# Computing the modulation vectors of a two-block network with column-grouped matmuls instead of row sums on VectorE

## The reference

```
def modulation(cvec, w, b):
    m = jax.nn.silu(cvec) @ w + b
    return jnp.split(m, 3, axis=-1)

def modulate(n, shift, scale):
    return n * (1.0 + scale) + shift
...
        shift, scale, gate = modulation(c, mod_w[i], mod_b[i])
        h = modulate(rmsnorm(x, norm_g[i]), shift[:, None], scale[:, None])
        ...
            shift_c, scale_c, gate_c = modulation(c_ctx, mod_w[i], mod_b[i])
        ...
        x = x + gate[:, None] * y
```

## Time and profile before

| what | us |
|---|---|
| median of 3 runs | 3019.34 (3016.89 to 3021.15) |
| the profiled execution, its own time | 3007.58 |
| span of the profiled execution | 3005.8 |
| PE busy | 2610.2 (87%) |
| PE weight loads busy | 2028.2 (67%) |
| DVE busy | 1748.8 (58%) |
| ACT busy | 1122.0 (37%) |
| POOL busy | 776.2 (26%) |

### The profile page before, as it was taken

One profiled execution on the slowest core, in us unless ns is written; L12 is line 12 of the kernel. 1 busy time (PEld: TensorE's weight loads), 2 busy tenths in 40 slices (PEclk: granted clock), 3 DMA queues, 4 the chain that ended last, 5 costly groups with the idle time before them and its releaser, 6 DMA issues. The chain is left out here.

```text
span 3005.8 us, 65971 instructions
## 1 busy us (share of the span) xinstructions
PE 2610.2 (87%) x28252; PEld 2028.2 (67%) x28252; DVE 1748.8 (58%) x2951; ACT 1122.0 (37%) x1751; POOL 776.2 (26%) x437
## 2 busy tenths in 40 slices
PE   7896879998599997788888888678999999898987
PEld 5774658776487686677677777567778755476755
DVE  4646978977822675454554554354771066535995
ACT  4531332223333422444444443332442344333323
POOL 2322210001122123644444452122332300032111
PEclk9998989989698898899999999889999999999998
DMA  4214424432234455111111100324332200033431
GB/s 149 77 43 133 161 71 118 111 93 91 97 107 151 157 188 182 40 36 45 51 40 46 51 25 14 122 91 147 133 126 64 84 1 1 1 119 92 136 94 56
DMA packets 83662, 266.34 MB, mean 89 GB/s; under 512 B 11824, under 2 KB 12848, under 8 KB 82992
## 3 DMA queue, kind: packets, MB, share of 16 engines
q1 hardware_dynamic: 74160, 236.97, 24.8%
q10 hardware_dynamic: 9216, 25.17, 2.1%
HBM read 203.04 MB, written 36.70 MB: 80 GB/s over the span
## 5 line engine op out<-in xcount | busy, mean ns | idle before, releaser
L358 PE MATMUL ps<-h_parts_conv,w_parts_conv 128*128 128x512 f32 x3936 | 766.5, 356 | 83.7 <-DVE h_parts_conv L344 47.6
L358 PEld LDWEIGHTS ps<-h_parts_conv,w_parts_conv 128*128 128x128 f32 x3936 | 643.2, 193 | 212.9 <-issue 54.7
L358 PE MATMUL ps<-scratch_scan 64*64 64x64 f32 (+1 forms) x15936 | 379.8, 239 | 82.9 <-issue 44.5
L358 PEld LDWEIGHTS ps<-scratch_scan 64*64 64x64 f32 x15936 | 342.9, 140 | 127.5 <-issue 83.6
L355 ACT ACTIVATE scratch_scan<-ps 128x384 f32<-128x384 f32 x560 | 241.0, 493 | 370.5 <-PE ps L358 228.4
L358 PE MATMUL ps<-h_parts_attn,w_parts_attn 128*128 128x512 f32 (+1 forms) x1536 | 330.5, 374 | 19.9 <-DVE h_parts_attn L352 12.3
L352 DVE SCALAR_TENSOR_TENSOR scratch_conv<-scratch_conv,vec 128x256 f32<-128x256 f32 (+1 forms) x672 | 335.2, 572 | 0.5
L358 PEld LDWEIGHTS ps<-h_parts_attn,w_parts_attn 128*128 128x128 f32 x1536 | 264.6, 191 | 78.6 <-issue 15.2
L432 POOL TENSOR_TENSOR w_parts_conv<-ring,w_parts_conv 128x1024 fp32r<-128x1024 f32 x50 | 131.4, 2629 | 592.2 <-ACT w_parts_conv L355 592.2
L358 PE MATMUL ps<-h_parts_block,w_parts_block 128*128 128x512 f32 x960 | 243.7, 414 | 38.5 <-POOL w_parts_block L432 27.7
L358 PEld LDWEIGHTS ps<-h_parts_block,w_parts_block 128*128 128x128 f32 x960 | 189.4, 200 | 92.4 <-issue 42.8
(11 more groups left out here) (206 smaller groups left out, 3586.0 us busy)
## 6 DMA issues: line engine op xcount, KB each, us to landing
ring<-in_weights SPq DMA_DIRECT2D x311, 512.0 KB, 3.7
rwkv_spill<-scratch_conv ACTq DMA_DIRECT2D x64, 384.0 KB, 2.3
stream<-rwkv_spill SPq DMA_DIRECT2D x64, 384.0 KB, 4.0
scratch_conv<-scratch_conv SPq DMA_DIRECT2D x128, 103.1 KB, 2.2
scratch_conv<-scratch_conv SPq DMA_DIRECT2D x128, 67.4 KB, 2.0
x_spill<-stream SPq DMA_DIRECT2D x2, 3072.0 KB, 9.7
y_spill<-scratch_scan SPq DMA_DIRECT2D x8, 384.0 KB, 4.0
scratch_rwkv_out<-y_spill SPq DMA_DIRECT2D x8, 384.0 KB, 6.5
```

Source lines behind the costliest of these rows:

```text
L358: return nc.tensor.matmul(o, l, r, start=start, stop=stop)
```

## The change

All 96 blocks become kind `mod` and are laid out as 128 inputs by 1024 outputs. A "third" is the 8 blocks that make 1024 outputs (shift, scale or gate) of one layer; there are 12. For each block `mod_block` issues four matmuls in float32, one for each column group of 32: the weights are 32 columns of `SCW` (the two conditions of input tile k and 30 further columns of the same buffer), the moving data 256 outputs from the ring, the result 32 partitions by 256 columns of one PSUM bank, accumulated over the 8 blocks. The ring slot is now released by PE. After the eighth block ACT copies 128x256 out (`mod_copy`), PE turns it to the layout with outputs on partitions by 8 matmuls with two moving columns each (`mod_turn`), and DVE adds the bias (`mod_add`, one operation for all 8 tiles).

`MODS_AT` places the blocks of a third after tiles 1 to 6 of a group of eight: 2, 2, 1, 1, 1, 1. The thirds now stand in `in1` (two), `out1`, `gate1`, `convout0` (one each), `rkvg` (three, in k, v and g), `attn_qk` (three), `attn_g` (one). In `in1` ACT's copy of the direct block `rg` is moved ahead of `round_block`. `spread_conditions`, the DVE copies of it, `mod_rows`, `mod_bias` and the PE block at the end of `conv0` go.

```diff
-PE_MODS = range(8, 14)
+MODS_AT = {1: 2, 2: 2, 3: 1, 4: 1, 5: 1, 6: 1}
...
+        due = {first + m: n for first in mods for m, n in MODS_AT.items()}
         for n, b in enumerate(body):
             plan.append(b)
-            plan.extend(("mod_w_2", layer, k) for layer, k in (mods or {}).get(n, ()))
+            for _n in range(due.get(n, 0)):
+                plan.append(("mod_w_2", third[0] // 24, third[0] % 24))
+                third[0] += 1
...
+        def mod_block(pe, bank):
+
+
+            s, k, third = R.take_mod(pe)
+            if k == 0 and third:
+                pe.wait_ge(mods_added, third)
+            for j in range(4):
+                last = mm(PS[32 * j:32 * j + 32, bank * 512:bank * 512 + 256], SCW[:, 2 * k:2 * k + 32], RINGT[:, s, 256 * j:256 * j + 256],
+                          k == 0, k == DT - 1)
             last.then_inc(mod_done, 1)
...
+        def mod_copy(a, third, bank, rows):
+
+            a.wait_ge(mod_done, DT * (third + 1))
+            act(rows, PS[:, bank * 512:bank * 512 + 256], ACT.Copy).then_inc(rows_copied, 1)
+
+        def mod_turn(pe, third, bank, rows):
+
+            pe.wait_ge(rows_copied, third + 1)
+            for m in range(DT):
+                j, h = m // 2, m % 2
+                a = bank * 512 + 256 + 2 * m
+                last = mm(PS[:, a:a + 2], rows[:, h * P:h * P + P], C("ident")[:, 32 * j:32 * j + 2])
+            last.then_inc(mods_turned, 1)
...
                     tile_product(pe, PS[:, (m % 2) * 1024:(m % 2) * 1024 + width], width,
                                  fresh=(split_low, base_low, 1) if split and m == 0 else None)
+                        if mods:
+                            for _n in range(MODS_AT.get(m, 0)):
+                                mod_block(pe, mods[1])
+                    if mods:
+                        mod_turn(pe, *mods)
                     S.total(pe)
...
                     tensor_taps(pe, DT - 1)
-                    if j_ == 0:
-                        pe.wait_ge(b_read, past + DT)
-                        for n in PE_MODS:
-                            mod_block(pe, n)
                     pe.wait_ge(a_read, past + DT)
...
                 for m in range(DT):
-                    if m < 6:
-                        mod_rows(v, CB, JUNK, (0, 1))
-                        mod_rows(v, CB, JUNK, (0, 1))
                     v.wait_ge(g_read, m + 1)
```

More of the change, by code:

```diff
@@ L121, in weight_plan @@
     in1 = [("w_in", 0, m) for m in IN_ORDER]
-    stage("in1", in1[:2] + [("rg", 0, 0)] + in1[2:])
-    stage("out1", [("w_out", 0, m) for m in range(8)], {m: [(0, 2 * m), (0, 2 * m + 1)] for m in range(6)})
+    stage("in1", in1[:2] + [("rg", 0, 0)] + in1[2:], (1, 11))
+    stage("out1", [("w_out", 0, m) for m in range(8)], (0,))
     stage("gate1", [("w_ple_proj", 0, 0), ("w_ple_proj", 0, 1)] + [("w_ple_gate", 0, m) for m in range(8)],
-          {3 + m: [(0, 12 + 2 * m), (0, 13 + 2 * m)] if m < 2 else [(1, 2 * m - 4), (1, 2 * m - 3)] for m in range(6)})
+          (2,))
@@ L133, in weight_plan @@
     stage("rkvg", rkvg[0] + lora[0] + rkvg[1] + lora[1] + rkvg[2] + rkvg[3],
-          {20 + 8 * q + m: [late[12 * q + 2 * m], late[12 * q + 2 * m + 1]] for q in range(2) for m in range(6)})
+          (10, 20, 28))
     stage("rwkvout", [("rwkv_w_o_2", 0, m) for m in range(8)])
-    stage("attn_qk", [("attn_w_in_2", 0, m) for m in QK_ORDER], {m: [(2, 16 + m)] * (m < 8) + [(3, m)] for m in range(24)})
+    stage("attn_qk", [("attn_w_in_2", 0, m) for m in QK_ORDER], (0, 8, 16))
     stage("attn_v", [("attn_w_in_2", 0, 24 + m) for m in range(8)])
-    stage("attn_g", [("attn_w_in_2", 0, 32 + m) for m in range(16)])
+    stage("attn_g", [("attn_w_in_2", 0, 32 + m) for m in range(16)], (0,))
@@ L381, in two_blocks @@
[L381 to L389, removed]
-        def mod_bias(layer, first, n):
-            b = V("mod_b_2", 24 * layer + first, n).rearrange("p (m o) -> p m o", o=1).broadcast_to([P, n, 2])
-            dlink(vtt(MODL[:, layer, first:first + n], PMOD[:, first:first + n], b, ALU.add))
@@ L1109, in _ @@
                     last.then_inc(p_done, 1)
+                    for _n in range(MODS_AT.get(m, 0)):
+                        mod_block(pe, 5)
+                mod_turn(pe, 3, 5, MOD_ROWS)
                 S.total(pe)
@@ L1553, in _ @@
                         n += 1
-                        if kind == "v" and m == 0:
-                            pe.wait_ge(cb_ready, 3)
-                            spread_conditions(pe, CB_PS, (1,))
+                        if kind in "kvg":
+                            for _n in range(MODS_AT.get(m, 0)):
+                                mod_block(pe, 7)
+                            if m == DT - 1:
+                                mod_turn(pe, 5 + "kvg".index(kind), 7, MOD_ROWS)
                     if prods[0][0] == "lora":
@@ L1602, in _ @@
                 for n, (kind, q, m) in enumerate(seq):
+                    if kind in "kvg" and m == DT - 1:
+                        mod_copy(a, 5 + "kvg".index(kind), 7, MOD_ROWS)
                     if kind not in "wa":
```

168 lines of the change are left out of this document (73 added, 95 removed).

## The result

| | before | after |
|---|---|---|
| median, us | 3020.59 (3016.89 to 3030.01, 20 runs) | 3031.95 (3021.08 to 3040.22, 20 runs) |
| ratio | | 1.0034, 95% interval 1.0025 to 1.0043 |
| the profiled execution | 3007.58 | 3036.78 |

What follows compares the result with a forecast made beforehand. PE was taken to bound the unbroken runs of tiles, with pauses elsewhere; stage terms -16.3 - 21 - 6.5 + 2.5 - 3.1 + 18.6 + 11.2 = -14.6 us gave 3019.3 - 14.6 = 3004.7 us, range 2984 to 3020.

Steps and rivals of the forecast that it cites:

- Prices on PE: Each block on PE: 0.43 us streaming plus 0.17 entry; single 0.60, pair 1.03, third 4.5, turn 1.7 us.
- serial rival: Also "one after another": column groups sharing the ring run serially, 1.15 us x 96 = 110; 3090 us, slower; chance 0.04.
- The new wait: PE waits before tile 3 for weights loaded behind the pair: 1.5 us at 512 positions, none at 768.
- Attention, +18.6: Attention projections: first k tile -10.5, other thirds and turns +17.4, norm waits +4, attn_g +7.7; 18.6 us longer.
- in1, +11.2: in1: first third, wait and turn 7.7 us; second third hidden by a pause, but 2 us shift and 1.7 turn.
- out1 and gate1: Pauses come back in both stages, less the blocks' cost: out1 21 us shorter, gate1 6.5 us shorter.
- conv0, -16.3: End of conv0: channel sums start sooner, ending the stage 15.4 us earlier, plus 0.9 without the next stage's spread.
- rkvg, -3.1: rkvg: k pays a third and turn, +6.2 us; v and g gain 9.3 us from pauses.
- The sum against the median: Profiled execution 3007.6 - 14.6 = 2993.0 us; its 11.8 us below the runs' median carried over, giving 3004.7.
- More comes back: Rival: waits behind pairs may be hidden, out1 and gate1 tails shrink by 2; -28 us, 2991; chance 0.20.
- The clock: Rival: eight exposed turns and six waits each cost a 1.6 us clock lapse; +8 us, 3027, slower; chance 0.13.
- The ring feeds PE badly: Rival: 48 single blocks hold ring slots until PE reaches them, 0.2 us each, +10; 3014 us; chance 0.13.

Runs made afterwards that it cites:

- with the buffers aligned: The changed kernel with 32 instead of 30 unused floats, so later buffers stand 128 instead of 120 bytes further than before; ratio 1.0028 to the kernel before.
- The form with one pair: The changed kernel with each third's blocks placed 2,1,1,1,1,1,1 from the first tile on (gate stage unchanged); 3024.42 us, ratio 1.0013.
- the kernel with short sums: The kernel before with one matmul instead of eight for each of six direct blocks at conv0's end; 2997.36 us (ratio 0.9939), again 2999.26 (0.9922).

## Why the prediction was wrong

- **What bounds the kernel: right.** In the stages that were unbroken runs of tiles the blocks are paid in full; in those with pauses time came back.
- **Prices on PE: the step that failed first.** A single block is 0.78 instead of 0.60, a pair 1.24 instead of 1.03, a third with its turn 7.4 instead of 6.2. The streaming (0.43) was right, the entry was not: 0.35 us instead of 0.17. The taps follow one another in one long entry, and I had shared their time between streaming and switching by an assumed 3.84 us that no row gave. Over the eight thirds in in1, convout0, rkvg's k and attention this is 10 us. (The same term was left out of the serial rival: 1.75 - 0.43 is 1.32 us a block, not 1.15.)
- **The new wait: right in place, small in size.** In the profile it is 3.5 (in1), 1.5, 2.9 (out1), 0.8 (gate1) and 3.8 us (attn_g), where 1.5 to 1.9 was reckoned, since a load behind a pair lands 6.6 to 6.9 us after it (in1, attn_g), with the other load beside it, not 4.5. The tile behind such a wait may run 1.6 to 2.9 us longer, and the length of the wait does not say whether: in the profiles of the changed kernel, with the buffers aligned too, tiles took 7.34 and 7.31 us behind 2.13 and 2.45, but 5.72 and 5.70 behind 2.86 and 3.10. The form with one pair shows that most of it can be avoided.
- **Attention, +18.6: +30.** The first k tile came back as reckoned (PE went on to it at 2033.14, 1.0 us behind tile 1's end; 10 us, with the first pair in it). Against that stand four thirds at 7.4, the wait in attn_g with its slow tile (3.8 and 2.9), and 5.6 us for the last norm, a line of the diff that I had read as a replacement for an old wait and put at nothing. It was worth more than any error of size in this stage. The two waits for a norm inside the thirds, put at 4 us, were one of 1.9 us in the first profile and 0.3 in the second.
- **in1, +11.2: +16.** Two thirds at 7.4, waits of 3.5 and 1.5 us and 1.6 for the longer tile are 21.5. The pause ahead of the recurrence shrank only from 8.35 to 6.56 us, so it hid 1.8 and not a whole third; and a wait of 2.3 us that the kernel before had in this stage, with 1.6 for the tile behind it, is gone.
- **out1 and gate1: right** (-18.0 for -21, -5.8 for -6.5); the difference is the entries and the wait of 2.9.
- **conv0, -16.3: -12.9.** 14.0 at its end: the channel sums come 16.2 us sooner, as forecast, but the squares' sums of the next stage stand behind a new pause of 3.98 us and take 12.3 and 13.5 us against 10.5. The slower last taps take 1.7 back; the pause and the slower squares' sums are about made up for by channel sums of 11.4 us instead of 13.3 and by the spread of 3.7 that is gone. The rest is the first profile of before with its shorter tiles; against the other two the stage is 14.1 us shorter.
- **rkvg, -3.1: +3.7.** k +9.9 for +6.2 (906.1 to 992.3 for nine tiles): 7.4 for the third and its turn, a wait of 0.4, and 2 that are within chance, since the same nine tiles, 76.31 us in my base profile, took 79.18 in the kernel with short sums, whose code there is that of before. v and g -4.7 for -9.3.
- **The sum against the median: wrong.** I took the 11.8 us between profile and median for a property of the kernel; three profiles of it lie 13.0 (11.8 by the three runs that I had), 7.1 and 0.0 us under the medians beside them. The 31 runs of the kernel before beside the first experiments lie from 3006 to 3031 us, and only one of them is under the 3007.6 of my base profile: it was a short one by luck. By the stages the changed kernel is 20 us longer, by the runs 5 to 10. With two and three profiles such a spread can make the difference, but that is argued; part of it may be the open point at the end of conv0.
- **Rivals.** "More comes back" and "one after another" are out. "The clock" was right only behind some of the waits: tiles behind turns and blocks ran at 5.67 to 5.78. "The ring feeds PE badly" was the nearest in kind, with the wrong place: behind pairs, not singles.

What would have given the sign: 8 thirds x 1.2 us and the norm's 5.6 alone turn -14.6 into +0.6.

## What to carry to other kernels

Work moved from an idle engine to the one that bounds the kernel pays only in stages where that engine has pauses which this work's old place caused; so move it stage by stage. Here four or five stages on PE and the rest on DVE give 0.9929 to 0.9938, all of it on PE 1.0018 to 1.0034. In1, 16 us longer with its two thirds, kept them on PE in every run; whether they too are better placed elsewhere was not tried. Price a short burst by a row of short bursts, with the growth of its neighbours, and read every wait in the diff for a round trip: an engine that waits for a value which it has just issued itself.

## What the runs showed of the hardware

- Four column groups of 32 stream fully side by side: 224 columns in each took 0.38 us together. Going in and out costs 0.35 us, some 0.2 of it in the tile beside the block (5.67 us for 5.46).
- The same 144 fp32r matmuls of three 768-position tiles take 25.2 or 25.7 us, constant over a stretch, without a pattern that these runs show.
- 96 narrow matmuls (`128x2`, two records each) took 39.05 us, 48 of them 16.4 to 16.6. The granted clock was 1.00 (2.4 GHz) over the first 2.2 us of the 96, and over the first 4 of the 48; then it fell to 0.50 (1.2 GHz) while PE was issuing them, and stayed there to their end. PE's last pause, 3.2 to 3.3 us, lay ahead of the taps before them.
- A load of 512 KB with another one beside it landed 6.6 us (in1) and 6.9 us (attn_g) after the pair of blocks whose slots they took, where the median from issue to landing of all ring loads is 4.3.
